# Another instruction order for the chunk scan of an RWKV-7 layer, on four engines

## What is computed

```
def step(s, inp):                      # s: (heads, value 64, key 64)
    r_t, w_t, k_t, v_t, aa_t, bb_t = inp
    sa = einsum('bhij,bhj->bhi', s, aa_t)
    s = s * w_t[:, :, None, :] + sa[..., None] * bb_t[:, :, None, :] + v_t[..., None] * k_t[:, :, None, :]
    return s, einsum('bhij,bhj->bhi', s, r_t)
s_last, ys = lax.scan(step, s0, (r_h, w_h, k_h, v_h, -kk, kk * a_h))   # kk: k * k_k, divided by its norm over a head
```

## Time and profile before

| | |
|---|---|
| median of 3 executions | 3142.97 us (3138.88 to 3146.47) |
| span of the profiled execution | 3144.1 us, 1.1 us over the median |
| chunk scan in it | 1652 to 2138 us after the start |
| PE busy over the span | 3010.5 us, 96% |
| DVE, ACT, POOL busy | 1805.6, 1023.8, 965.1 us |

### The profile page before, as it was taken

One profiled execution on the slowest core, in us unless ns is written; L12 is line 12 of the kernel. 1 busy time (PEld: TensorE's weight loads), 2 busy tenths in 40 slices (PEclk: granted clock), 3 DMA queues, 4 the chain that ended last, 5 costly groups with the idle time before them and its releaser, 6 DMA issues.

```text
span 3144.1 us, 66739 instructions
## 1 busy us (share of the span) xinstructions
PE 3010.5 (96%) x29234; PEld 2891.6 (92%) x29234; DVE 1805.6 (57%) x1884; ACT 1023.8 (33%) x1281; POOL 965.1 (31%) x549
## 2 busy tenths in 40 slices
PE   8999999999999997889998999998999999999998
PEld 7899999999999997889997777887999999999997
DVE  7766765555656557512206777773566555565657
ACT  6533411111111113633326667764311111111113
POOL 1322223222222223313314555552132322222221
PEclk9999999999999999999998999999999999999999
DMA  3111111111111111242232222213111111111111
GB/s 107 46 44 41 39 44 41 48 48 41 48 41 48 41 48 34 81 174 86 90 110 73 70 69 71 75 48 102 41 48 41 41 48 48 41 48 41 48 41 71
DMA packets 88684, 185.66 MB, mean 59 GB/s; under 512 B 29024, under 2 KB 53088, under 8 KB 88416
## 3 DMA queue, kind: packets, MB, share of 16 engines
q1 hardware_dynamic: 81504, 154.73, 15.6%
q10 hardware_dynamic: 6912, 26.84, 2.1%
HBM read 145.01 MB, written 36.53 MB: 58 GB/s over the span
## 4 chain that ended last, share of the span: by engine, by line
PE 78%; DVE 14%; ACT 5%; issue 1%; POOL 1%; DMA 1%; DVEq 0%; SPq 0%; ACTq 0%; POOLq 0%
PE PS L1306 64%; PE PS L1516 10%; DVE T L1764 3%; DVE X L1764 2%; DVE T L1779 2%; PE PS L1442 2%; ACT T L512 2%; DVE BK L1764 1%; DVE HL L1774 1%; ACT L512 1%; DVE G L1764 1%; PE PS L1396 1%; DVE T L1774 1%; ACT UV L512 1%; PE PS L1358 1%
## 5 line engine op out<-in xcount | busy, mean ns | idle before, releaser
L1089 POOL TENSOR_TENSOR WL<-RAW,WH 128x1024 fp32r<-128x1024 f32 x204 | 496.0, 2432 | 1393.4 <-ACT WH L512 1389.5
L1306 PE MATMUL PS<-HH,WH 128*128 128x364 f32 x3456 | 771.8, 331 | 31.9 <-DVE HL L1774 12.7
L1306 PE MATMUL PS<-HH,WL 128*128 128x364 f32 x3456 | 767.4, 330 | 0.0
L1306 PE MATMUL PS<-HL,WH 128*128 128x364 f32 x3456 | 764.3, 330 | 0.0
L1306 PEld LDWEIGHTS PS<-HH,WH 128*128 128x128 f32 x3456 | 601.1, 189 | 41.5 <-issue 15.8
L1306 PEld LDWEIGHTS PS<-HH,WL 128*128 128x128 f32 x3456 | 605.7, 189 | 0.0
L1306 PEld LDWEIGHTS PS<-HL,WH 128*128 128x128 f32 x3456 | 603.0, 189 | 0.0
L512 ACT ACTIVATE WH<-RAW 128x1024 fp32r<-128x1024 f32 x204 | 216.7, 1062 | 825.9 <-PE PS L1306 809.6
L1764 DVE TENSOR_TENSOR T<-PS,T 128x1092 f32<-128x1092 f32 x110 | 142.6, 1296 | 552.4 <-PE PS L1306 535.6
L1764 DVE TENSOR_TENSOR X<-PS,X 128x1092 f32<-128x1092 f32 (+2 forms) x240 | 292.8, 1220 | 235.1 <-PE PS L1306 216.6
L1306 PE MATMUL PS<-PH,WH 128*128 128x364 f32 x1248 | 278.2, 331 | 10.2 <-DVE X L1764 5.2
(11 more groups left out here) (191 smaller groups left out, 3458.8 us busy)
## 6 DMA issues: line engine op xcount, KB each, us to landing
RAW<-weights SPq DMA_DIRECT2D x204, 512.0 KB, 3.3
scratch<-T ACTq DMA_DIRECT2D x31, 546.0 KB, 3.1
scratch<-SR ACTq DMA_DIRECT2D x14, 546.0 KB, 2.9
X<-xT SPq DMA_DIRECT2D x8, 546.0 KB, 7.7
T<-scratch_m SPq DMA_DIRECT2D x8, 512.0 KB, 3.7
KK<-scratch SPq DMA_DIRECT2D x16, 192.0 KB, 2.9
LW<-scratch SPq DMA_DIRECT2D x16, 192.0 KB, 2.8
AA<-scratch SPq DMA_DIRECT2D x16, 192.0 KB, 3.2
```

Source lines behind the costliest of these rows:

```text
L1089: pool.tensor_tensor(out, full, hi, ALU.subtract).then_inc(*t.made(event))
L1306: mm = pe.matmul(acc[:, j, :], a, b[:, j * CW:(j + 1) * CW], start=(i == 0 and q == 0), stop=(i == len(blocks) - 1 and q == 2))
```

## The change

The scan's arithmetic stays as it is. Three things differ.

1. The four sums are cut into matmuls of 64 columns (`sum_of`), 12 or 10 for a batch in the place of 2. Those of the key squares alternate with the left products of level 3; the other three stand alone.
2. A link is cut into `link_state(i)` and `link_out(i)`, which are placed apart. The spread now alternates with the left products of level 5, and the products of 128 columns with which it alternated stand alone (`lower_alone`).
3. The order of the calls is another one on PE, DVE and ACT, and on POOL one pair is exchanged.

```diff
# ACT
                 turned_removal()
-                scaled_key()
-                decay_in()
+                key_factor()
...
                 centred_square()
...
                 solved_values()
                 solved_keys()
-                key_square()
+                decay_in()
                 turned(1)
                 growth()
+                scaled_key()
                 group_ln()
-                key_factor()
+                key_square()
+                values()
                 turned(2)
-                values()
                 norm_ln()
-                group_exp()
...
                 turned(3)
-                norm_exp()
+                group_exp()
                 affine()
...
                 turned(4)
+                norm_exp()
                 outputs_y()
# POOL
                 grown_taken()
+                grown_key()
                 receptance()
-                grown_key()
# PE
-                def sums(src, event, reader, count):
+                def sums_bank(reader, count):
...
-                        mul(PS[HALF[h], 2, 0:src.shape[-1]], CO[HALF[h], C_BD + h * CHUNK:C_BD + (h + 1) * CHUNK],
-                            src[HALF[h]], event)
+                        mul(tile(2, h, i), CO[HALF[h], C_BD + h * CHUNK:C_BD + (h + 1) * CHUNK],
+                            src[HALF[h], (at + i) * CHUNK:(at + i + 1) * CHUNK], event if i == n - 1 else None)
...
+                def left_and_key_squares():
+
+                    left_begin(3)
+                    key_squares_begin()
                     for i in range(6):
+                        left(i)
+                        key_square_of(i)
...
                 variances()
+                left_and_moves()
                 fresh_state()
-                moves_and_left(2)
+                grow(2)
+                link_state(0)
+                value_turn()
+                left_and_key_squares()
                 fresh_out()
-                grow(2)
-                key_squares()
-                link(0)
-                left_times(3)
-                link(1)
-                value_turn()
-                link(2)
                 grow(3)
-                link(3)
+                link_out(0)
+                link_state(1)
                 products(0)
-                left_times(4)
-                link(4)
+                link_out(1)
+                left_alone(4)
+                link_state(2)
+                link_out(2)
                 bonus_sums()
                 products(1)
-                link(5)
+                link_state(3)
                 grow(4)
+                link_out(3)
                 key_turn()
-                left_times(5)
-                lower_and_spread()
+                link_state(4)
+                link_out(4)
+                left_and_spread()
+                link_state(5)
+                link_out(5)
+                lower_alone()
                 grow(5)
# DVE
                 near()
-                scan()
                 centred()
                 one_more()
+                scan()
                 grown(1)
                 removal()
+                mask(2)
+                reading()
+                transfer()
+                key()
+                grown(2)
                 grown_half()
-                mask(2)
-                transfer()
-                reading()
-                grown(2)
+                mask(3)
+                floor()
                 state(0)
-                key()
+                weighted()
+                grown(3)
                 state(1)
-                mask(3)
+                masked(0)
                 state(2)
-                floor()
-                grown(3)
-                weighted()
-                state(3)
-                masked(0)
-                state(4)
                 mask(4)
                 masked(1)
+                state(3)
                 grown(4)
+                state(4)
+                mask(5)
                 bonus()
                 state(5)
-                mask(5)
```

More of the change, by code:

```diff
@@ L1542, in means @@
                         held(("k_ys", job))
-                        sums(flat(Y)[:, na * CHUNK:nz * CHUNK], "s_mean", "k_cent", job)
+                        sums_bank("k_cent", job)
+                        for i in range(nz - na):
+                            sum_of(flat(Y), na, i, nz - na, "s_mean")
                 def variances():
@@ L1548, in variances, with bonus_sums_begin, bonus_of @@
                         held(("k_csq", job))
-                        sums(Q1[:, na * CHUNK:nz * CHUNK], "s_var", "k_gln", job)
-                def bonus_sums():
+                        sums_bank("k_gln", job)
+                        for i in range(nz - na):
+                            sum_of(Q1, na, i, nz - na, "s_var")
+                def bonus_sums_begin():
                     if has_p:
                         held(("k_prep", q + 1))
-                        sums(X3[:, pa * CHUNK:pz * CHUNK], "s_bon", "k_bonus", q + 1)
+                        sums_bank("k_bonus", q + 1)
+                def bonus_of(i):
+                    if has_p and pa + i < pz:
+                        sum_of(X3, pa, i, pz - pa, "s_bon")
                 def solved():
@@ L1699, in key_turn, with lower_begin, lower @@
                                 mm.then_inc(*t.made("k_tb"))
-                def lower_and_spread():
+                def lower_begin():
                     if has_p:
                         held(("k_bkt", q + 1), ("k_eye", 1))
+                def lower(i):
+                    if has_p and pa + i < pz:
+                        for h in range(HEADS):
+                            mul(PAIR[HALF[1 - h], i * P:(i + 1) * P], AR[HALF[h], pa + i, 0, :],
+                                BK[HALF[h], pa + i, 2 * h::3 - 2 * h, :], "k_l0" if pa + i == pz - 1 else None)
@@ new lines, in left_and_key_squares, with left_alone, bonus_sums @@
+                def left_and_key_squares():
+                    left_begin(3)
+                    key_squares_begin()
+                    for i in range(6):
+                        left(i)
+                        key_square_of(i)
+                def left_alone(k):
+                    left_begin(k)
+                    for i in range(6):
+                        left(i)
+                def bonus_sums():
+                    bonus_sums_begin()
+                    for i in range(6):
+                        bonus_of(i)
@@ L1717, in interval, with left_and_spread, lower_alone @@
+                def left_and_spread():
+                    left_begin(5)
+                    spread_begin()
+                    for i in range(6):
+                        left(i)
+                        spread(i)
+                def lower_alone():
+                    lower_begin()
+                    for i in range(6):
+                        lower(i)
                 means()
```

76 lines of the change are left out of this document (43 added, 33 removed).

## The result

The changed kernel takes 3172.9 us in the median (3163.33 to 3177.63) against 3144.57 in the same comparison, a ratio of 1.0089 with a 95% interval of 1.0074 to 1.0105. It is slower, and outside the range of the forecast; it lies inside the 3164 to 3184 us of rival C. The profiled execution is the shortest of the four, 3163.33 us with a span of 3161.5, and that of before, 3144.1, is the longest of its own. The two traces therefore account for 17.4 of the 28.3 us between the medians.

What follows compares the result with a forecast made beforehand. PE and the chains of waits through it were taken as the bound; 23 intervals of -0.33 us work and -0.5 us waits make -19, code +3, so -16 us to 3127 us, range 3113 to 3149.

Steps and rivals of the forecast that it cites:

- rival C: PE runs dry at most packet borders, +40 to +60 us against -19: 3164 to 3184 us; chance 0.11 with anything like it.
- the key squares: Alternating with level 3 left products they save 0.61 us an interval; the two together wait 0.15 us for ACT's chain.
- the term for code: PE's instruction packets over the scan: 12% more is +1 us, taken as +3, with bounds 0 and +20.
- Schedule and work: In each scan interval, work changes by -0.33 us and waits by -0.5.
- the waits and the order: PE's waits for other engines fall from 1.8 to 1.3 us an interval, 0.5 less.
- the other sums: The other three sums cost 0.75 us each in pieces instead of 0.65, +0.28 us an interval.
- B before `grow(2)`: PE's 0.39 us of idle time for DVE's B goes, as the mask precedes BK and the fresh state covers it.
- W: After the solve, left products and moves on PE wait about 0.3 us for ACT's W, a new wait.
- BK: DVE's BK, 1.39 us beside POOL's own BK, keeps 1.39 us beside POOL's `grown_key` and `receptance`.
- B and D: Rivals: B, ACT's chain runs late, 3140 to 3146 us; D, waits as now, 3138 us; together 0.23.
- the last 0.03: The chance left for an unseen wait at the edges, half of it slower.

Runs made afterwards that it cites:

- e1_all_wide: The changed kernel with all four sums whole again, the key squares ahead of the left products of level 3; 3137.83 us.
- e3_before_cut: The kernel before, in its own order, with all four sums in 64-column pieces; 3171.74 us.
- e2_squares_cut: The changed kernel with only the key squares in pieces and the other three sums whole; 3147.88 us.
- e5_half_code: On e1_all_wide, one 128-column matmul for two neighbouring chunks in powers, level 4 left products and grow, so values differ; 3109.72 us.
- e4_before_waits: The kernel before with 150 waits that are long satisfied added in each interval on PE; 3204.93 us.
- e6_before_mask: The kernel before with the mask of level 2 put ahead of BK on DVE; 3146.76 us.
- e7_all_full: On e1_all_wide, each sum as one matmul over 128 rows and the products with weights of 128 columns; 3144.82 us.
- e10: The kernel before with the products of 128 weight columns, two matmuls for four; 3142.69 us.

## Why the prediction was wrong

**The step that failed** is the term for code. It scaled the breaks of before by the packets ("12% more packets is +1 us", taken as +3). They went from 7.9 to 48.7 us, +41, beyond the +20 of its bound. The breaks did not grow in proportion to the packets, 104 to 116 in the 22 intervals: both parts of the change raised the demand, more records and fewer waits, and the stops are what the supply falls short of it. e1_all_wide shows the second part alone (+14.0 us of breaks at equal code), e3_before_cut the first (+24.4 at the old order); both together gave +40.8, about their sum. Rival C, which got 0.11, had the mechanism and its evidence, dense blocks and 12 matmuls for 2; its own figure, some 43 breaks of 0.6 us more than before as the point of decision, was passed with 48 more at 0.79 on average (48.7 / 62). What I held against it, that nine intervals before had only 5.8 us of "issue", was a reading at the demand of the old order; in e1_all_wide, at the same number of records, the breaks were 21.9 us.

**Schedule and work** were forecast at -0.83 us an interval; without breaks it was -0.65. By its terms: the waits and the order -0.58 (e1_all_wide) for -0.5, the key squares -0.26 (e2_squares_cut) for -0.61, the other sums +0.19 for +0.28.
- *B before `grow(2)`*: right. B,MT starts behind the fresh state with no idle time, where the earlier trace rows has 0.39, and the loads' waits for B and G went.

```profile
1764.54 0.27 PE L1516 MATMUL PS<-B,MT 64*64 64x64 f32 x2
```

- *W*: forecast 0.3, and it came with this releaser: 4.9 us in 10 cases, 0.43 in the interval shown. It is short in the sum because breaks often cover it; in e5_half_code, without breaks, it is 9.0 / 22 = 0.41.
- *Key squares*: they alternate as forecast, the pair in 0.86 us (1766.09 to 1766.95) for 0.76. Their wait is not visible. But their gain was 0.26 us an interval by e1_all_wide and e2_squares_cut without breaks, not 0.61; the longer pair is 0.1 of the difference, and the rest these runs do not explain.

```profile
1766.09 0.27 PE L1516 MATMUL PS<-M,G 64*64 64x64 f32 x2
1766.10 0.27 PE L1516 MATMUL PS<-X,CO 64*64 64x64 f32 x2
1766.17 0.25 PE L1516 MATMUL PS<-M,G 64*64 64x64 f32 x2
...
1766.95 0.28 PE L1516 MATMUL PS<-G,UV 128*64 128x64 f32 x2
```

- *The other three sums*: that of the means took 0.70 us to the start of `powers` at 1758.54, against 0.75 forecast; 0.28 an interval was forecast for all three; from e2_squares_cut to after the interval without breaks grew by 0.19.

```profile
1757.84 0.87 PE L1516 MATMUL PS<-Y,CO 64*64 64x64 f32 x24
```

- *BK*: the row was kept at 1.39 us, and it was too long. Measured over the run (min/median/max):

```profile
L1847 DVE TENSOR_TENSOR BK<-X,Z x24: 490/860/3051, 1647.9 to 2121.6; 64x384 f32<-64x384 f32 x16, 64x320 f32<-64x320 f32 x8
```

and beside POOL in the interval shown:

```profile
1766.02 0.86 DVE L1847 TENSOR_TENSOR BK<-X,Z 64x384 f32<-64x384 f32 x1
...
1765.47 1.00 POOL L1187 TENSOR_TENSOR BK<-KK,Z 128x384 f32<-128x384 f32 x1 [1.12 <-DVE KK L1847]
```

DVE began in the middle of POOL's instruction, which ended at 1766.47, and was done 0.41 us behind that, after 0.86 us in all; in the kernel before the two began within 0.02 us of one another, and DVE's took 1.39. The median fell from 1381 to 860 ns. What it saved does not show beside the breaks.

**What the sum left out** is the start. In the profiled runs, the first line before and the second after, the stretch from 1652 to 1680 ran at a mean granted clock of 0.70 and of 1.00:

```profile
1652.00:1680.00 28.00, 20.50 (x432) 16.22 (x436) 14.64 (x21) 13.08 (x21) 11.26 (x11) 0.70 0.27 89
```

```profile
1652.00:1680.00 28.00, 20.16 (x692) 17.64 (x684) 17.26 (x27) 15.95 (x29) 12.63 (x13) 1.00 0.28 85
```

The first interval took 20.6 to 21.6 us in the profiled runs of before, e3, e4, e6, e7 and e10, and 17.0 to 17.5 in all the others. e7 has the new order, so the order of engines alone doesn't decide it; what does is open. It is worth 4 us, about half of e1_all_wide's gain. Nor does a kernel seem to fix it. 28 us at 0.70 lower the mean clock of a whole run by 0.003, and executions of one kernel differ by that much: of the ten of e1_all_wide nine have 0.990 or 0.991, and one has 0.986 and is the slowest with 3145.65 us; of the ten of e7_all_full six have 0.990 to 0.992 (3137.41 to 3145.12 us) and four 0.987 to 0.989 (3147.28 to 3148.97). So a few microseconds between these medians can be how many executions started slowly.

One sum in the chances is off: 0.03 of B and D, 0.11 of C and half of the last 0.03 make 0.155 for slower, where it has 0.14.

## What to carry to other kernels

Before you cut matmuls into small pieces or close PE's last waits, count its instructions per microsecond as you would count bytes. Here the breaks of "issue" inside blocks, 62 in after and some 126 matmul records or a multiple of that apart, were the sign that their supply was near its limit, a packet in 3.93 us. From there a wait removed can come back as a stop: e1_all_wide got nothing of its 0.58 us an interval. Then the same columns in fewer instructions can be worth more than a better order, if the wide form costs PE less than the stops do: here the products in the new order (1.09 us for 0.90 in a group of four chunks, and 3129.98 us for 3137.83), but not in the old one (a ratio of 1.0000 to before), and not the sums (0.84 us for 0.65). And an instruction moved ahead in a queue wins little if the next wait for the same queue grows: e6_before_mask took 7.6 us from the loads' waits for B and added 5.4 to those for M.

## What the runs showed of the hardware

In the profile each float32 matmul of the scan stands as two records, each with a weight load: the value turn has 12 matmuls for a batch of six chunks and 10 for one of five, 272 over the 24 jobs, and IST,VV has 544 matmul records and 544 loads, in before as in after. A matmul on 64 rows and 64 columns has the form 64*64 there, and no form in the 14 traces is larger than 128*128, four times that; a "quarter" is one such part. Matmuls on different quarters ran beside one another: 24 records of left products took 0.75 us from start to start on two quarters, and the 48 of `grow(2)` 0.76 on four; in after, 20 records of left products alternating with 24 of key squares, these on the other two quarters, took 0.86 (1766.09 to 1766.95).

PE's code came in packets of 16 KB, 252 records of matmuls and loads each in after. In none of the 14 traces did two of them start less than 3.25 us apart within the 22 intervals, and the mean went no lower than 3.93, in after. After a break PE resumed 2.4 us behind the start of the latest packet in the median of after (2.2 to 3.0; medians of 2.35 to 2.75 in all traces), and the next packet started 1.3 us after PE had resumed (medians of 1.3 to 1.7). The packet itself was under way for 1.0 us of that in the median. The 2.4 and 1.3 us make 3.7, near the pace of after, as if a packet were fetched only when PE had gone on into the one before; that is argued from these times and not tested. A block on all four quarters uses a packet's 126 matmul records in about 2 us (an estimate from 48 in 0.76), which is why breaks could come in e1_all_wide too, whose mean demand, a packet in 4.16 us, is slower than that pace.

Weights of 128 columns cost the products 1.09 us for 0.90 in a group of four chunks, and a sum over all 128 rows took 0.84 us for 0.65 (384 columns, e7_all_full for the earlier trace rows): in both, half the instructions took about 0.2 us longer. A wait that is long satisfied took PE some 11 ns (1.62 us for 150, e4_before_waits).
